# A two-block sequence model on one core: gated linear attention kept token-major, and the local attention's key and value weights packed into one unit

## The reference, cut to what matters

```python
# gated linear attention, a head h at a time; chunks of C = 64 tokens
bcum = cumsum(log_sigmoid(glr @ w_gk2 + b_gk) / 16, inside the chunk)
q_t = q * 128 ** -0.5 * exp(bcum);  k_t = k * exp(-bcum)
o_intra = tril(q_t @ k_t.T) @ v                 # inside the chunk
k_dec = k * exp(b_last - bcum)
o_inter = q_t @ S                               # S is the state before the chunk
S = S * exp(b_last) + k_dec.T @ v               # 128 x 256, once for each chunk
o = rms_norm(o_intra + o_inter) * g_onorm * silu(gate)
h = h + o @ w_out
# local attention
k, v = split(rmsnorm(h, kv_norm) @ w_kv, 2)     # 128 columns each: 2 heads of 64
s = q @ k.T / 8 + bias(distance, head)          # head i uses key head i // 8
p = exp(s - m) / (sum(exp(s - m)) + exp(sink - m));  h = h + (p @ v) @ w_out
```

## Time and profile before

| | us |
|---|---|
| three runs, median (lowest to highest) | 2472.6 (2470.88 to 2474.7) |
| profiled execution, device time | 2472.28 |
| profiled execution, span | 2470.5 |
| PE busy in it | 2421.8 (98%) |
| DVE busy | 1476.8 (60%) |
| ACT busy | 873.5 (35%) |

### The profile page before, as it was taken

One profiled execution on the slowest core, in us unless ns is written; L12 is line 12 of the kernel. 1 busy time (PEld: TensorE's weight loads), 2 busy tenths in 40 slices (PEclk: granted clock), 3 DMA queues, 4 the chain that ended last, 5 costly groups with the idle time before them and its releaser, 6 DMA issues.

```text
span 2470.5 us, 28869 instructions
## 1 busy us (share of the span) xinstructions
PE 2421.8 (98%) x11238; PEld 1986.0 (80%) x11238; DVE 1476.8 (60%) x2038; ACT 873.5 (35%) x1158; POOL 22.1 (1%) x37
## 2 busy tenths in 40 slices
PE   8999999999999999999999899999999999999998
PEld 7887878788888877788887688888888877888886
DVE  6988745644445845544445734656665776655666
ACT  4444544422222743422223533422222465321222
POOL 0000000000000000000000000000000000000000
PEclk9999999999999999999999999999999999999999
DMA  5222222323222322222322221233333212222321
GB/s 189 94 86 92 97 68 83 108 92 102 102 85 85 103 68 69 85 87 100 102 94 82 90 98 52 70 109 106 120 107 121 102 52 69 88 100 102 102 85 68
DMA packets 38892, 229.19 MB, mean 93 GB/s; under 512 B 8821, under 2 KB 8837, under 8 KB 12448
## 3 DMA queue, kind: packets, MB, share of 16 engines
q1 hardware_dynamic: 31824, 220.22, 26.4%
q0 software_dynamic: 6992, 7.92, 1.3%
HBM read 222.82 MB, written 5.24 MB: 92 GB/s over the span
## 4 chain that ended last, share of the span: by engine, by line
PE 89%; DVE 6%; ACT 3%; issue 1%; DMA 0%; DVEq 0%; SPq 0%; ACTq 0%
PE bank L691 88%; DVE w_lo L1918 1%; ACT w_hi L1377 1%; DVE xs L2028 1%; ACT xs L1459 1%; DVE xs L2048 1%; PE bank L1316 1%; ACT xh L1396 0%; DVE xl L1933 0%; DVE sum_x L1940 0%; ACT pr L1646 0%; DVE spare_lo L1915 0%; DVE cacc L2153 0%; DVE sum_q L1947 0%; DVE xs L2004 0%
## 5 line engine op out<-in xcount | busy, mean ns | idle before, releaser
L1918 DVE TENSOR_TENSOR w_lo<-w_raw,w_hi 128x2048 fp32r<-128x2048 f32 x201 | 460.4, 2291 | 382.0 <-ACT w_hi L1377 381.8
L691 PE MATMUL bank<-xh,w_hi 128*128 128x512 f32 x1416 | 559.7, 395 | 16.1 <-DVE w_lo L2317 6.8
L691 PE MATMUL bank<-xl,w_hi 128*128 128x512 f32 x1416 | 554.2, 391 | 0.0
L691 PE MATMUL bank<-xh,w_lo 128*128 128x512 f32 x1416 | 554.0, 391 | 0.0
L1377 ACT ACTIVATE w_hi<-w_raw 128x2048 fp32r<-128x2048 f32 x201 | 383.5, 1908 | 384.2 <-PE bank L691 384.1
L2004 DVE TENSOR_TENSOR xs<-xs,bank 128x512 f32<-128x512 f32 x448 | 294.1, 683 | 100.4 <-PE bank L691 99.4
L691 PEld LDWEIGHTS bank<-xh,w_hi 128*128 128x128 f32 x1416 | 268.0, 189 | 79.1 <-issue 12.4
L691 PEld LDWEIGHTS bank<-xl,w_hi 128*128 128x128 f32 x1416 | 268.0, 189 | 56.4 <-issue 1.2
L691 PEld LDWEIGHTS bank<-xh,w_lo 128*128 128x128 f32 x1416 | 267.7, 189 | 56.4
L691 PE MATMUL bank<-yh,w_hi 128*128 128x512 f32 x576 | 227.1, 394 | 0.4 <-DVE w_lo L1918 0.3
L691 PE MATMUL bank<-yl,w_hi 128*128 128x512 f32 x576 | 224.3, 389 | 0.0
(11 more groups left out here) (284 smaller groups left out, 2948.4 us busy)
## 6 DMA issues: line engine op xcount, KB each, us to landing
w_raw<-weights_in SPq DMA_DIRECT2D x205, 1024.0 KB, 4.9
rel_scratch<-vt POOLq DMA_DIRECT2D x8, 384.0 KB, 20.0
bias<-rel_scratch POOLq DMA_DIRECT2D x8, 256.0 KB, 3.1
y_out<-xs SPq DMA_DIRECT2D x8, 256.0 KB, 2.1
xs<-x_in SPq DMA_DIRECT2D x3, 512.0 KB, 8.0
mk<-mem_in POOLq DMA_DIRECT2D x1, 1024.0 KB, 8.1
window<-consts_in POOLq DMA_DIRECT2D x1, 576.0 KB, 6.6
xs<-x_in SPq DMA_DIRECT2D x2, 256.0 KB, 4.2
```

The costliest lines, as they stand in the source:

```text
L691: return pe.matmul(dst, a, b, start=start, stop=stop)
L1918: dve.tensor_tensor(w_lo[:, c % 2, :], w_raw[:, c % 2, :], w_hi[:, c % 2, :].bitcast(F32), ALU.subtract)\
```

## The change: what it does

Gated linear attention becomes a function of its own on each engine (`gated_attention`), local attention gets one unit for keys and values (`skv`), and the units are 205 in all.

1. Output token-major. Masked scores are now the stationary operand and the values stream, 4 calls of 256 columns. For the state, `kT` holds the transposed keys without zeros; a chunk's call contracts over its 64 rows only, with chunk 2t in rows 0 to 63 and chunk 2t+1 in rows 64 to 127, each into a bank of its own. Across chunks the queries of one chunk (64 columns) are the stationary operand and the state streams with 256 columns into output partitions 0 to 63 or 64 to 127.
2. The norm. The sum of squares of a token comes from ACT (Square with an accumulated sum, two calls of 256 columns for each half of the tokens), Ln and Exp work on 128 x 2 values, and ACT scales the rows on the way out into `osc`. PE then transposes `osc` to feature-major (8 transposes, `feature_major`), and DVE multiplies by gain and gate straight from PSUM. The squares' matmul and DVE's multiplication by the root go.
3. Order. Two state steps, then the second half of the products inside the chunks and `feature_major` of the head before; then across and state steps in turn; the next head is opened before the last two `across_chunks`.
4. `skv` = `wide(kv)`: 128 key columns, 128 value columns, 48 matmuls in place of 72. Query heads are paired as hp and hp+8 (weights of `sq` and `so` reordered on the host), so keys need no doubling. DVE makes `yl` for six tiles, adds the squares, then makes the last two.
5. `side(n)` and a last load keep banks and SP's loop right with an odd number of units.

```diff
+def side(n):
+    return (n + (n > UNITS["skv"])) % 2
...
+            def gated_attention():            # PE
...
+                def within_chunks(h, half):
+                    key = ("gla", "o", h, half)
+                    wait_free(pe, key)
+                    for s in range(2):
+                        t = 2 * half + s
+                        mm(bank(key)[:, s * 2 * P:(s + 1) * 2 * P], sum_x[:, t * P:(t + 1) * P],
+                           gv[:, t, h * 2 * P:(h + 1) * 2 * P], s == 0, False)
+                def state_steps(h, t):
+                    for c in range(2):
...
+                        full(mm(bank(key)[:, 0:2 * P], kT[r, t * P:(t + 1) * P],
+                                gv[r, t, h * 2 * P:(h + 1) * 2 * P], True, True), key)
+                def across_chunks(h, t):
...
+                        wait_drained(pe, ("gla", "ds", h, i - 1))
+                        last = mm(bank(key)[64 * c:64 * c + 64, (t % 2) * 2 * P:(t % 2 + 1) * 2 * P], gq[:, h, i * 64:(i + 1) * 64],
+                                  gs[:, (i % 8) * 2 * P:(i % 8 + 1) * 2 * P], False, t % 2 == 1)
...
+                def feature_major(h):
+                    for half in range(2):
+                        wait_drained(pe, ("gla", "o", h, half))
+                    for d in range(2):
...
+                            last = pe.transpose(bank(key)[:, t * P:(t + 1) * P], osc[:, t, d * P:(d + 1) * P], ident[:, :])
...
+                open_head(0)
+                for h in range(HEADS):
+                    wait_drained(pe, ("gla", "scores", h))
+                    within_chunks(h, 0)
+                    wait_drained(pe, ("gla", "kend", h))
+                    state_steps(h, 0)
+                    state_steps(h, 1)
+                    within_chunks(h, 1)
+                    if h:
+                        feature_major(h - 1)
+                    across_chunks(h, 0)
+                    state_steps(h, 2)
+                    across_chunks(h, 1)
+                    state_steps(h, 3)
+                    if h + 1 < HEADS:
+                        open_head(h + 1)
+                    across_chunks(h, 2)
+                    across_chunks(h, 3)
...
             def head_tile(k):
+                if k == 2:
+                    last_head(HEADS - 1)
                 tile_ready(k)
-                if k == 1:
-                    head_squares(HEADS - 1)
...
-            feature_unit("sk", 0, ready=tile_ready)
-            c = UNITS["sv"]
...
+            feature_unit("skv", 0, ready=tile_ready)
...
+                def scaled_rows(h, half):         # ACT
+                    key = ("gla", "o", h, half)
+                    r = rinv[:, h % 2, 2 * half:2 * half + 2]
+                    wait_full(act, key)
+                    for s in range(2):
+                        t = 2 * half + s
+                        last = act.activation(osq[:, s, :], bank(key)[:, s * 2 * P:(s + 1) * 2 * P], ACT.Square,
+                                              accum_out=rsum[:, h % 2, t:t + 1])
+                    steps.step(last)
+                    steps.wait()
+                    steps.step(act.activation(r, rsum[:, h % 2, 2 * half:2 * half + 2], ACT.Ln, scale=1.0 / (2 * P), bias=eps[:, :]))
+                    steps.wait()
+                    steps.step(act.activation(r, r, ACT.Exp, scale=-0.5))
+                    steps.wait()
+                    for s in range(2):
+                        t = 2 * half + s
+                        last = act.activation(osc[:, t, :], bank(key)[:, s * 2 * P:(s + 1) * 2 * P], ACT.Copy,
+                                              scale=rinv[:, h % 2, t:t + 1])
+                    free(last, key)
...
+                prepare(0)
+                last_values()
+                for h in range(HEADS):
+                    drain(("gla", "kend", h), kT[:, :], bank(("gla", "kend", h))[:, :])
+                    if h + 1 < HEADS:
+                        prepare(h + 1)
+                    if h:
+                        scaled_rows(h - 1, 1)
+                        outputs(h - 1)
+                    scaled_rows(h, 0)
+                scaled_rows(HEADS - 1, 1)
+                outputs(HEADS - 1)
...
+                for h in range(HEADS):            # DVE
+                    if h:
+                        wait_drained(dve, ("gla", "ds", h - 1, 2 * TT - 2))
+                    if h + 1 < HEADS:
+                        prepare(h + 1)
+                    state_steps(h, 0)
+                    state_steps(h, 1)
+                    if h:
+                        gated(h - 1)
+                    state_steps(h, 2)
+                    state_steps(h, 3)
+                    if h:
+                        outputs(h - 1)
+                    if h + 1 < HEADS:
+                        masked_scores(h + 1)
+                gated(HEADS - 1)
+                outputs(HEADS - 1)
...
-            for k in range(KT):
+            for k in range(6):
                 give(rest(k, xs[:, k, :], col("mix2_g1", k), yh, yl), "tile_ready")
-            split_lo(UNITS["sv"] + 1)
             for k in range(1, KT):
                 add_to_sums(k, False, xs_at, late=0)
+            for k in range(6, KT):
+                give(rest(k, xs[:, k, :], col("mix2_g1", k), yh, yl), "tile_ready")
...
-           "sk": wide(np.concatenate([kv[:, 0:64], kv[:, 0:64], kv[:, 64:128], kv[:, 64:128]], axis=1)),
-           "sv": narrow(kv[:, 128:256]), "sq": wide(i["b_w_q_2"][0]), "so": wide(i["b_w_out_2"][0])}
+           "skv": wide(kv), "sq": wide(i["b_w_q_2"][0].reshape(D, 2, 8, 64).transpose(0, 2, 1, 3).reshape(D, D)),
+           "so": wide(i["b_w_out_2"][0].reshape(2, 8, 64, D).transpose(1, 0, 2, 3).reshape(D, D))}
```

More of the change, by code:

```diff
@@ L145, in pair @@
         n = UNITS[stage] + j
-        fill((stage, j, 0), 2 * (n % 2))
-        fill((stage, j, 1), 2 * (n % 2) + 1, n)
+        fill((stage, j, 0), 2 * side(n))
+        fill((stage, j, 1), 2 * side(n) + 1, n)
     def pairs(stage, n):
@@ L164, in gla @@
         for h in range(HEADS + 1):
-            if h < HEADS:
-                fill(("gla", "scores", h), 4)
-                fill(("gla", "kend", h), 5)
-            if h:
-                fill(("gla", "ssq", h - 1), 3)
-            if h == HEADS:
-                break
-            fill(("gla", "o", h, 0), 6)
-            fill(("gla", "o", h, 1), 7)
-            for t in range(TT):
-                fill(("gla", "ds", h, t), t)
+            if h:
+                for d in range(2):
+                    fill(("gla", "oT", h - 1, d), 4 + d)
+            for head in (0, 1) if h == 0 else (h + 1,):
+                if head < HEADS:
+                    fill(("gla", "scores", head), 4)
+                    fill(("gla", "kend", head), 5)
+            if h < HEADS:
+                fill(("gla", "o", h, 0), 6)
+                fill(("gla", "o", h, 1), 7)
+                for i in range(2 * TT - 1):
+                    fill(("gla", "ds", h, i), i % 4)
     def linear_attention(name, filler):
@@ L238, in ups @@
             c += 1
-        b = 2 if gated else 2 * ((UNITS[name] + (tag != "first")) % 2)
+        b = 2 if gated else 2 * (side(UNITS[name]) ^ (tag != "first"))
         return f + [((name, tag, "u", 0), b, None), ((name, tag, "u", 1), b + 1, c)]
@@ L530, in build @@
         mh = sb(second, "mh", [P, 2, 2, T])
-        kend_gla = sb(alias, "kend_gla", [P, TT, 2 * P])[:, :, :]
+        kT = sb(alias, "kT", [P, TT * P])
+        osq = sb(alias, "osq", [P, 2, 2 * P])
+        osc = sb(alias, "osc", [P, TT, 2 * P])
         alias.close()
@@ L632, in _ @@
                       .then_inc(raw_loaded[s], 16)
+            if N_UNITS % 2:
+                sp.wait_ge(w_lo_ready, N_UNITS - 2)
+                load(0, N_UNITS - 1)
             for k in range(KT):
@@ L1247, in _ @@
             chunks("mlp0", tile_and_sums("r1"))
-            feature_unit("sk", 0, ready=tile_ready)
-            c = UNITS["sv"]
-            pe.wait_ge(w_lo_ready, c + 1)
-            wait_free(pe, ("sv", 0, 0))
-            for k in range(KT):
-                last = mm3(bank(("sv", 0, 0))[:, :], weights(c, k * P, P), xtile(k), k == 0, k == KT - 1)
-            full(last, ("sv", 0, 0))
+            feature_unit("skv", 0, ready=tile_ready)
             qv = sf[:, :].rearrange("p (k t) -> p k t", k=KT)
@@ L1618, in linear_attention, with gated_attention, prepare, outputs @@
                 outputs(HEADS - 1)
+            def gated_attention(last_values):
+                def prepare(h):
+                    if h == 0:
+                        seen.next("b_ready", HEADS)
+                    if h:
+                        seen.next("kq_ready")
+                        wait_full(act, ("gla", "kend", h - 1))
+                    give(act.activation(geb[:, :], gb[:, h, :], ACT.Exp, scale=1.0 / 16.0), "eb_ready")
+                    give(act.activation(genb[:, :], gb[:, h, :], ACT.Exp, scale=-1.0 / 16.0), "eb_ready")
+                def scaled_rows(h, half):
```

(9 more changed lines are left out.)

114 lines of the change are left out of this document (91 added, 23 removed).

## The result

| | kernel before | changed kernel |
|---|---|---|
| median of six runs, us | 2472.6 (2470.9 to 2474.7) | 2459.2 (2456.75 to 2460.7) |
| profiled execution / its span, us | 2472.3 / 2470.5 | 2457.0 / 2455.2 |

The ratio is 0.9948 with the interval [0.9937, 0.9958]. The forecast was 2461.3, in a range of 2456.5 to 2466.5: it holds, and the kernel gained 2.1 us more than the sum had.

The account below looks back on a forecast made before the run. PE, busy 98%, was taken to bound the kernel, with ACT's norm next in linear attention. From 2472.3 us, less 6.6 for linear attention and 4.6 for the shared unit, came 2461.1, set at 2461.3 for the runs' median; range 2456.5 to 2466.5.

Parts of the forecast that it names:

- PE's own head: Linear attention: PE's own work for a head falls to 9.2 us, where 11.2 stood.
- The nine changes: Linear attention: switches between whole and half array cost 0.2 us each, 1.8 a head, range -0.6 to +0.6.
- The ring: Linear attention: PE 3.8 us plus ACT 6.4, through the bank the norm must free, give a period of 10.2.
- second branch: Linear attention: transposes, gating on DVE (2 x 0.7) and two ACT splits, of nearly the same length as PE's part.
- The end of the stage: Linear attention: output projection at 39.1 us, first output unit ends at 51.4, before 58.0; gain 6.6.
- The unit: Shared keys and values: 24 matmuls less, 5.44 us, minus a 0.8 wait; gain 4.6, between 3.5 and 5.4.
- the slower case: Linear attention: the norm's order reloads ACT's table, 1.28 us each, two for each half; 2481.9 us, chance 0.03.
- Without pairing: Linear attention: calls wait for their own states and don't pair, PE 2.6 us a head more; 2468.6, chance 0.09.
- PE does not set the pace: Denies a rival: in linear attention ACT's halves take 2.1 us, so PE's 9.2 limits; 2458.3, chance 0.2.
- the longer ring over DVE: Linear attention: accumulate and scaled copy cost more, or DVE's turn adds, 1 us a head; 2465.3, chance 0.17.

Follow-up runs that it names:

- The shorter norm: Changed kernel with the two accumulated squares of each half replaced by one small ACT operation on two columns; 2457.8 us, one run.
- the first comparison: Changed kernel against the kernel before, medians of six runs: 2459.2 against 2472.6 us, ratio 0.9948.
- the kernel with the eight remainders first: Changed kernel with DVE making all eight tiles of yl before it adds the squares, not six; 2460.1 us, one run.

## Why the prediction was right

- **PE's own head.** Predicted 9.2, measured 9.02. State and across chunks pair (1.07 and 1.02 for eight records with their change of mode). The nine changes, taken at 0.2 each, cost 0.09 to 0.21, 1.5 in all and not 1.8. The changes between half rows and half columns, which no row showed, are like the others: from 1524.62 to 1525.25 four records in pairs, 0.43, and one change, 0.20; from 1525.25 to 1525.83 the other way, 0.15.
- **The ring.** PE waits where it was predicted to, ahead of the second half inside the chunks, released by the norm's last copy, and ACT's norm, key copy and exponentials are in the ring. The other side of the ring was wrong: in heads 1 and 2 it closes over DVE's products, state steps and gating and ACT's splits, and not over PE's blocks. The prediction had gating and splits as a second branch "of nearly the same length", beginning at PE's transposes, and did not price it; DVE comes to the gating behind its products and state steps, and that way is the longer by 0.1 us. The shorter norm shows it: it took 0.67 us from the period, one half's worth, and not two. Where the state and across blocks take the whole array, or the next head is opened last, the ring does close over PE and ACT. The sizes were off both ways: from the first Square to the free bank 5.94 us for 6.4, from there to the next Square 4.0 for 3.8. That the period came out at 9.95 for 10.2 is in part luck, as the two errors have opposite signs. Most of ACT's is the accumulated square, for which the prediction took the distance of 0.46 between two other operations with a sum; the squares stand 0.36 apart, and a half takes 2.29 for 2.45.
- **The end of the stage.** The output projection begins at 38.5 for 39.1: the first head releases its bank at 13.6 for 13.95, the periods are 9.95 and 9.33 for 10.2 and 9.45, the rest 5.6 for 5.4. The last transposes, predicted to wait 0.35 in the first output unit, did not wait (1549.84 to 1550.63, 0.79). Together these are the 1.0 us by which linear attention brought more than 6.6.
- **The unit.** 24 matmuls less are 5.44, less a wait predicted at 0.8 and measured at 0.78 by starts: 4.66, and 4.60 arrived for 4.6. The order on DVE, six remainders and then the sums, is worth at least 1.3 us of it.
- **The rivals.** No table load appears in the stage, so the slower case had no start. Without pairing PE's block of eight would have taken 1.73; the pairs take 0.86 and a change. PE does not set the pace: it waits 0.9 us a head, where the prediction looked for 1.0 to 1.2. Of the longer ring over DVE the mechanism is there and the price is not: 0.1 us a head and not 1.

Of the 13.4 us between the medians of the first comparison 12.2 are accounted for by distances. The other 1.2 is within what the clock does from run to run, and no experiment here separates it further.

## What to carry to other kernels

When an engine is nearly full and work is taken from it, price two things: its own new sum, with 0.1 to 0.2 us for each change between whole and half array, and the longest ring through the other engines; the longer of the two is the period. Price every branch of that ring that looks nearly as long, and follow it in the trace by starts until it closes: here every wait of PE in heads 1 to 3 named ACT, while DVE was in the ring and PE was not. A reordering that removes the wait in sight must be followed once around the other engines' orders, since here it uncovered a longer ring at once. And gains of a few us are measured by distances between the same events in traces with the same granted clock, not by whole runs alone.

## What the runs showed of the hardware

- The granted clock fell to its lower level for stretches though PE was 98% busy: 0.95 over 150 to 220 us in one trace of the kernel before and 1.00 in the changed kernel's, 0.93 over linear attention in another (3.3 us), 0.90 over 17 us in the kernel with the eight remainders first (1.6 us, right behind a wait of 1.93 us). Which stretch it hits differs from run to run.
- Packing half-size matmuls pays little when they alternate with whole ones: nine changes of mode took 1.5 us of the 2.6 that six pairs saved. From the whole array to half columns it was 0.09 us, between the other modes 0.15 to 0.21.
- A Square of 128x256 out of PSUM with its sum has a step of 0.36 us on ACT, though its record and that of the read of its sum add up to 0.62: lengths of neighbouring records overlap, and only steps may be added.
